# A two-layer network with an RWKV scan on one core: the chunk inverse as seven products by powers of one factor, in place of five levels of two products

## The reference, cut to what matters

```python
def _wkv_step(S, inp):
    r_t, w_t, k_t, v_t, a_t, b_t = inp
    sa = jnp.einsum('zbhvk,zbhk->zbhv', S, a_t)
    S = S * w_t[..., None, :] + sa[..., :, None] * b_t[..., None, :] + v_t[..., :, None] * k_t[..., None, :]
    return S, jnp.einsum('zbhvk,zbhk->zbhv', S, r_t)

def wkv_bidir(state0, scan_in):
    state, ys = lax.scan(_wkv_step, state0, scan_in)
    ys = jnp.moveaxis(ys, 0, 2)
    return state, ys[0] + ys[1][:, ::-1]
```

## Time and profile before

| | |
|---|---|
| median of 3 runs | 4044.05 us (4041.13 to 4046.62) |
| profiled execution, first to last instruction | 4039.7 us |
| busy: TensorE, VectorE, GpSimd, ScalarE | 92%, 58%, 33%, 30% |
| scan, from the first to the last head's body | 2812 to 3398 us |

### The profile page before, as it was taken

The page is one execution under the profiler, slowest core; times in us unless marked ns, Lnnn a source line. Parts: engine busy times, 40 slices in busy tenths (PEclk is TensorE's granted clock), DMA queues, the critical chain, the costliest instruction groups (busy, mean ns, idle before and its releaser), DMA issues. The chain is left out here.

```text
span 4039.7 us, 81581 instructions
## 1 busy us (share of the span) xinstructions
PE 3727.0 (92%) x32706; PEld 2683.2 (66%) x32706; DVE 2360.8 (58%) x3864; ACT 1204.0 (30%) x2668; POOL 1321.7 (33%) x1020
## 2 busy tenths in 40 slices
PE   8888999898999999899999997998999999899887
PEld 6667878657787898777344444874999998733333
DVE  4568882545985445565444445767888776623333
ACT  3352222344222322331111112224455454111112
POOL 4443444434445364573000000431555453000000
PEclk9999999999999999999999999999999999899999
DMA  4114542303554122345999995356333234589997
GB/s 128 56 53 170 184 157 93 104 1 105 178 187 146 66 96 75 99 138 228 404 420 420 420 420 212 134 177 201 88 89 91 78 93 147 199 366 422 421 421 316
DMA packets 231204, 787.80 MB, mean 195 GB/s; under 512 B 56008, under 2 KB 64024, under 8 KB 171136
## 3 DMA queue, kind: packets, MB, share of 16 engines
q1 hardware_dynamic: 225008, 764.12, 50.9%
q0 software_dynamic: 5328, 19.40, 1.2%
q10 hardware_dynamic: 576, 0.09, 0.0%
HBM read 736.15 MB, written 47.38 MB: 194 GB/s over the span
## 5 line engine op out<-in xcount | busy, mean ns | idle before, releaser
L2887 POOL DMA_INDIRECT moe0e_xg<-moe_h,moe_first_rows x20 | 18.9, 947 | 546.3 <-DVE moe_first_rows L3044 540.5
L3011 ACT ACT_TABLE_LOAD x32 | 41.1, 1283 | 519.2 <-PE moe1e_p_u L2957 262.4
L373 POOL TENSOR_TENSOR gmi_w_lo<-gmi_rows_w,gmi_w_hi 128x512 fp32r<-128x512 f32 x64 | 120.2, 1878 | 159.8 <-ACT gmi_w_hi L415 159.8
L3960 PE MATMUL scan_bank<-scan_T,scan_off 64*64 64x64 f32 x3840 | 159.4, 220 | 8.5 <-issue 5.7
L373 POOL TENSOR_TENSOR p_w_lo<-p_rows_w,p_w_hi 128x512 fp32r<-128x512 f32 (+3 forms) x88 | 113.5, 1291 | 159.9 <-ACT p_w_hi L415 159.9
L2887 POOL DMA_INDIRECT moe1e_xg<-moe_h,moe_first_rows x17 | 16.0, 940 | 451.0 <-DVE moe_first_rows L3044 444.4
L1159 POOL TENSOR_TENSOR f0u_w_lo<-f0u_w,f0u_w_hi 128x1024 fp32r<-128x1024 f32 x42 | 115.0, 2757 | 137.6 <-ACT f0u_w_hi L1175 137.6
L1159 POOL TENSOR_TENSOR f1u_w_lo<-f1u_w,f1u_w_hi 128x1024 fp32r<-128x1024 f32 x42 | 114.3, 2742 | 137.5 <-ACT f1u_w_hi L1175 137.5
L1227 DVE SCALAR_TENSOR_TENSOR f0u_ada<-hT,condition,f0u_ada 128x512 f32<-128x512 f32 x168 | 148.2, 949 | 16.4 <-DMA hT<-in_ada_w_dram 15.9
L1227 DVE SCALAR_TENSOR_TENSOR f1u_ada<-hT,condition,f1u_ada 128x512 f32<-128x512 f32 x168 | 140.5, 903 | 20.5 <-DMA hT<-in_ada_w_dram 20.0
L2984 PE MATMUL moe0e_p_y<-moe_ring,moe0e_gatedT 128*64 128x512 f32 x608 | 137.6, 605 | 7.8 <-ACT moe0e_gatedT L3013 7.8
(11 more groups left out here) (903 smaller groups left out, 11529.7 us busy)
## 6 DMA issues: line engine op xcount, KB each, us to landing
moe_ring<-in_moe_w_down_dram SPq DMA_DIRECT2D x140, 1024.0 KB, 18.0
gm_uT<-in_moe_w_gu_dram SPq DMA_DIRECT2D x111, 1024.0 KB, 16.6
moe_ring<-in_moe_w_gu_dram SPq DMA_DIRECT2D x102, 1024.0 KB, 24.7
walk_memory<-in_moe_w_gu_dram SPq DMA_DIRECT2D x60, 1024.0 KB, 24.4
hT<-in_ada_w_dram SPq DMA_DIRECT2D x48, 1024.0 KB, 6.8
f0u_w<-in_ffn_w_gate_up_dram SPq DMA_DIRECT2D x22, 1024.0 KB, 4.8
f1u_w<-in_ffn_w_gate_up_dram SPq DMA_DIRECT2D x22, 1024.0 KB, 4.8
gmi_rows_w<-in_ga_w_in_dram SPq DMA_DIRECT2D x64, 256.0 KB, 2.7
```

Source lines behind the costliest of these rows:

```text
L373: nc.gpsimd.tensor_tensor(w_lo[t % 2][:, 0:width], w[t % RAW][:, 0:width], w_hi[t % 2][:, 0:width], ALU.subtract).then_inc(w_lo_made, 1)
L2887: pool.indirect_dma_start(xg[:], None, H.h, bass.IndirectOffsetOnAxis(rows[:, 0:1], 0)).then_inc(gathered, 16)
L3011: nc.scalar.activation(sg[:], p_g[:], ACT.Silu).then_inc(silu_ready, 1)
L3960: mm = nc.tensor.matmul(out[r], lhsT[r], rhs[r], start=start, stop=stop, skip_group_check=True)
```

## The change

The inverse within 32-blocks is no longer built level by level. With R0 the start as before and N the entries of A that join blocks of 2 up to 32 (all four levels in one mask), F = N^T R0 stands for one factor, and the inverse of a 32-block is (1 + F)(1 + F^2)(1 + F^4)(1 + F^8) R0. Seven products of each group do the whole: FIRST makes F; three squaring stages multiply the power in Z by [power | R], which gives the next power and the addition to R at once; LAST_POWER multiplies R by the eighth power; OUTER and FINAL join the two 32-blocks as the old fifth level did. Up to there R is block diagonal and is kept folded, 64x32 instead of 64x64, beside the power in one tile WR of 96 columns. A squaring product so moves 96 columns, LAST_POWER 32, the others 64.

- TensorE: 21 products of four chunks in place of 30. The nine squaring products are issued as two half units of two chunks each, which makes 30 units again (UNITS), each with its walk part as before.
- ScalarE: a copy of F and of the outer Z (`copy_z`), and of each power to WR (`copy_power`): 15 copies, as before. The copy of a power comes before VectorE's addition, which waits for it.
- VectorE: 12 additions to the folded R (128x4x32), 3 of the old width, and 15 transposes behind the first three where there were 12.
- GpSimd: nine masks (`full`, `off`, `off_outer`) where there were 18; new are three folds of R (L3740 of the changed kernel) and, behind `kh`, three expansions of the folded R (L3748), on which the last transposes wait. The end factor `eed` is made behind them.

```diff
-    NZ = LEVELS * NG
+    NI = PRODUCTS * NG
+    FIRST, LAST_POWER, OUTER, FINAL = 0, 4, 5, 6
+    UNITS = [(n, part) for n in range(NI) for part in ((0, 4),) * (n // NG not in (1, 2, 3)) + ((0, 2), (2, 4)) * (n // NG in (1, 2, 3))]
...
+                    for g in range(NG):
+                        g4 = slice(4 * g, 4 * g + 4)
+                        pool.wait_ge(s["r_ready"], h * NG + g + 1)
+                        nc.gpsimd.tensor_tensor(WR[:, g4, folded], full[:, g4, 0:CH // 2], full[:, g4, CH // 2:CH], ALU.add).then_inc(s["r_folded"], 1)
...
                     if ahead is not None:
                         factors(ahead)
+                    for g in range(NG):
+                        g4 = slice(4 * g, 4 * g + 4)
+                        pool.wait_ge(s["r_added"], h * ADDED + adds_through(LAST_POWER * NG + g))
+                        nc.gpsimd.tensor_tensor(by_block(full[:, g4, :]), WR[:, g4, folded].rearrange("p c (o t) -> p c o t", o=1).broadcast_to([P, 4, 2, CH // 2]),
+                                                join[:, 3, :].rearrange("p (q o t) -> p q o t", q=1, o=2).broadcast_to([P, 4, 2, CH // 2]), ALU.mult).then_inc(s["r_full"], 1)
...
+                    for k, (n, (first, end)) in enumerate(UNITS):
+                        if n // NG in (FIRST, OUTER):
+                            copy_z(n)
+                        if squares(n) and end == 4:
+                            copy_power(n)
+                        walk_part(walk, k - 1)
+                        if ahead is not None and k % 2 == 0 and k:
+                            factor_part(ahead, k // 2 - 1)
...
+                    def turn_product(n):
+                        g4 = chunks(n)
+                        if n // NG == FIRST:
+                            dve.wait_ge(s["z_copied"], h * COPIED + copies_through(n))
+                            turn(WR[:, g4, power], Z[:, g4, :])
+                        elif squares(n):
+                            turn(Z[:, g4, :], WR[:, g4, power])
+                        elif n // NG == LAST_POWER:
+                            dve.wait_ge(s["r_full"], h * NG + n % NG + 1)
+                            turn(T[:, g4, :], full[:, g4, :])
...
+                            if stage == FIRST or stage == OUTER:
+                                mm = mmul(one(n)[:, q, :], stationary[:, j, :], T[:, j, :])
+                            elif squares(n):
+                                mm = mmul(wide(n)[:, q], stationary[:, j, :], WR[:, j, :])
+                            elif stage == LAST_POWER:
+                                mm = mmul(narrow(n)[:, q, :], stationary[:, j, :], WR[:, j, folded])
+                            else:
+                                mm = mmul(one(n)[:, q, :], stationary[:, j, :], full[:, j, :])
...
+                    for k, (n, (first, end)) in enumerate(UNITS):
+                        product(n, first, end)
+                        walk_part(k - 1)
```

More of the change, by code:

```diff
@@ L3442 @@
 GRID = 64
-LEVELS = 5
+BLOCK_BITS = 5
+PRODUCTS = 7
 LOG_DECAY = -math.exp(-0.5)
@@ L3712, in _ @@
+                    if ahead is not None:
+                        end_decays(ahead)
                 factors(0)
+                end_decays(0)
                 heads(body)
@@ L4129, in _ @@
+                    for k, (n, (first, end)) in enumerate(UNITS):
+                        product(n, first, end)
+                        walk_part(k - 1)
+                        if k == 0:
+                            pe.wait_ge(s["bon_read"], h + 1)
+                        if ahead is not None and k % 2 == 0 and k:
+                            factor_part(ahead, k // 2 - 1)
                 keep_clock(nc, S, bank[7][:, 0:P], 13)
@@ L4149, in rwkv_tables @@
     joins = []
-    for l in range(LEVELS + 1):
+    for l in range(BLOCK_BITS + 1):
         m = 1 << l
```

178 lines of the change are left out of this document (99 added, 79 removed).

## The result

The changed kernel takes 4003.8 us (median of 4 runs, 4000.1 to 4005.2) against 4045.1 on the same chip (4041.1 to 4046.6): ratio 0.9895, 95% interval 0.9881 to 0.9909. The later runs stand beside the kernel before on other chips, where it took 4040 to 4046 us; where a median and the ratio to the kernel before disagree by a few us, the ratio goes.

The account below looks back on a forecast made before the run. TensorE sets the pace, VectorE 14% behind. Ordinary heads 1.4, last head 1.5, first head 1.0 and stalls 2.3 sum to 6 to 7 us off the 4044.05 us median: 4037 us, range 4012 to 4058.

Parts of the forecast that it names:

- TensorE's work: Inverse products in a head's slots: 14.0 us before, 11.6 after, 2.4 us a head less; ends 0.7 and 4.2.
- Waits added: 0.6 + 0.7 + 0.8 + 0.2 = 2.3: Sum of (a) to (d), us a head; against 2.4 saved, an ordinary head gains 0.1 us.
- (a): First turn: TensorE's fourth unit waits for the turned first product behind VectorE's queue; 0.6 us a head, ends 0.3 and 1.0.
- (c): Expansion on GpSimd between narrow product and outer product makes TensorE wait 0.8 us a head; ends 0.4 and 1.6.
- (d): VectorE's factor product rk stands behind a turn and meets GpSimd's second expansion; 0.2 us a head.
- (b): Half units cover less of the walk's wait for ScalarE's copies behind factor activations; 0.7 us a head more.
- VectorE's total per head … no relief: VectorE's sums and turns in a head: 12.9 us before, 12.6 after, so no relief.
- R1: Rival, chance 0.15: waits land in existing stalls, TensorE's saving comes through; 4004 us, half 4024; sign: period under 35.5 us.
- The unexplained stalls: TensorE's 17.4 us of "issue" waits over the scan shrink with the 13% fewer matmuls: 2.3 us gained in all.
- Last and first head: Last head, without factor work, gains about 1.5 us; first head, without walk and set by VectorE, 1.0 us.
- R2: Rival, chance 0.15: ScalarE's factor activations set slots 4 to 10, so the kernel is slower, 4058 us.
- R3: Rival, chance 0.04: in the squaring products 96 columns cost like 128, 0.21 us a chunk; 4056 us.

Follow-up runs that it names:

- shift_late: The changed kernel with VectorE's shift moved from ahead of the first turn to behind the third: 4000.7 us, ratio to the kernel before 0.9901.
- wide128: The changed kernel with 128 instead of 96 moving columns in the nine squaring products (32 columns of zeros added): 4020.5 us, ratio to the kernel before 0.9927.
- split_product: The changed kernel with each 96-column product issued as one of 64 and one of 32 columns: 4048.9 us, ratio to the kernel before 1.0006.
- adds_first: The changed kernel with VectorE's addition ahead of ScalarE's copy of the power, which waits for it: 4054.7 us, ratio to the kernel before 1.0035.
- act_spread: The changed kernel with ScalarE's five factor activations in units 2, 6, 9, 13 and 16 instead of 2, 4, 6, 8 and 10: 4025.8 us.
- act_spread_shift: The changed kernel with act_spread's activation places and also VectorE's shift behind the third turn: 4030.0 us, ratio to the kernel before 0.9968.

## Why the prediction was wrong

- **TensorE's work, 2.4 a head less**: right. The 96-column chunk steps by 0.165 for my 0.164, the narrow one by 0.117; by the weight loads' busy time it is 2.15.
- **"Waits added: 0.6 + 0.7 + 0.8 + 0.2 = 2.3" failed**: 1.08 by idle time, 1.3 as 2.4 of work less 1.07 gained. (a) is 0.26; (c) and (d) are 0.6 to 0.8 together for 1.0; the waits for ScalarE's walk copies (b) rose from 14.6 to 21.4 us over the scan in the weight loads' list, 0.45 a head, not 0.7. Each was too high, by a fifth to more than a half. I had given each link its whole duration and a hand-over, while the rows overlap by 0.05 to 0.1 us from start to start (three turns in 1.08 us). And I added the waits up. shift_late and wide128 show that they cover each other: a wait taken out leaves 0.05 of 0.26, work put in comes out at about half its size. My sentence "every error of 0.5 us in one head's hand layout is 7 us" was right, but the range took these errors as free to cancel, and they all had one sign. This step is 1 us a head, 14 us.
- **"VectorE's total per head … no relief" failed**, and with it the case against R1 ("VectorE 21.5 busy"). I counted sums and turns alone. In the slots VectorE's busy time fell from 21.46 to 18.23 us: the bonus (0.86 us) now lies ahead of the slots, and the factor products with two SBUF inputs no longer run beside a long row of GpSimd masks. One of them, by groups over the scan, before and after:

```profile
L3832 DVE SCALAR_TENSOR_TENSOR scan_ka<-head_memory,head_cols 128x384 f32<-128x384 f32 x30 | 23.9, 797 | 0.0
```
```profile
L3875 DVE SCALAR_TENSOR_TENSOR scan_ka<-head_memory,head_cols 128x384 f32<-128x384 f32 x30 | 17.2, 574 | 0.0
```

  What share of TensorE's gain this is, no run shows.
- **"The unexplained stalls … 72 of some 554 matmuls a head go (13%): 2.3" failed**, and cost as much: 13 us by the matmuls' "issue" (14.8 to 1.8), 17 by the comparison with the packets. I scaled a stall that I didn't understand by the number of instructions. They are not proportional to it: 9% fewer packets (219 to 200) took 83% of the stalls (21 to 3.5 us), and putting the instructions back brought all of them back. The packets of the instruction queue were in the trace of before; I had not looked for them around the longest stall.
- **Last and first head**: 2.5 and 1.5 us gained for 1.5 and 1.0 forecast; right in sign and too small for the same reasons.
- **Rival R1** gave 4004 and the time is that, with the period of 34.5 us under my mark of 35.5. That its number fits is luck: it has 38 us of work come through whole and 2 more, and what came is 15 us from the slots of 14 heads, 18 from the stalls and 4 from the last and first head. The waits don't land in the stalls; they are half as large, and the stalls are mostly gone.
- **R2** exists in small, in units 6 to 12; **R3** is refuted by the chunk's 0.165, and 128 columns would have cost 13 to 17 us, about what its sum said.
- What I left out: the order of copy and addition, over 50 us. A prediction that weighs only what costs something misses what the change protects.

Still open: what share of the stalls in the kernel before is density and what traffic (9 of 21 us went with part of the traffic, against 5 by position alone), what VectorE's relief is worth, and why the clock falls in split_product.

## What to carry to other kernels

When a small-matmul stretch shows stalls in the middle of a run of matmuls that wait for nothing, look for a packet of the instruction queue 2 to 3 us ahead. Fewer, wider matmuls then gained twice here, and less traffic in that stretch went with fewer stalls. Between two engines that both take from one product, let the one go first behind which the walk's copies queue: here that was worth more than the whole change gained. And don't sum up waits of a hand layout: check which of them are at one time, and give errors of one sign their own place in the range.

## What was not expected of the hardware

- TensorE goes on from such a stall 2.2 to 3.0 us after a fetch of 16 KB of its program began (130 stalls of five kernels); the longest stall is 1.7 us.
- VectorE's rk, with its inputs in SBUF, ends 0.28 us behind the GpSimd instruction that it meets: 0.44 us alone, 0.56 where 0.28 of that instruction is left, 0.72 where 0.44 is, 2.02 where 1.74 is. `scan_bh` takes 0.51 alone and 1.61 where it meets `kh`, ending 0.41 behind it in 15 of 15 heads; the shift takes 0.38 and 0.94. Sums from PSUM and transposes take the same time either way (the squaring power's transpose 0.44).
- With the products split in 64 and 32 columns the granted clock went to half for 3.4 us in six of 15 walked heads. The kernels before and after have none there, adds_first has one, act_spread and act_spread_shift have two each; what brings it on stays open.
